# FFN of a six-stage network on one core: 512-column up products, down products two tiles behind, down weights loaded one tile later

## The chip, the cores and the metric

The kernel runs on 1 core of a Trainium2 chip. The metric is the device time in microseconds of that core. Before the change it is 1230.22 us, the median of 3 runs (1228.94 to 1235.15).

## The reference

The program is a chain of blocks on one sequence of 256 tokens with 1024 features: an attention mixer (MLA), FFN 0, a second mixer (diff), FFN 1, then FFN 2, a mixed block (sparse attention and a gated recurrence), FFN 3 and a last norm. All is in 32-bit floats. What is changed is the FFN, of which there are two kinds:

```python
def conv_ffn(x, w_up, conv_w, conv_b, w_down):   # FFN 0 and 1, 2816 hidden features
    u = x @ w_up                                  # gate half and value half side by side
    up = jnp.pad(u, ((0, 0), (1, 1), (0, 0)))
    c = conv_b
    for j in range(3):                            # 3 taps along the tokens
        c = c + conv_w[j] * up[:, j:j + s]
    g, val = c[..., :FFN_HIDDEN], c[..., FFN_HIDDEN:]
    return (jax.nn.gelu(g) * val) @ w_down

def swiglu(x, w_gu, w_down):                      # FFN 2 and 3, 2752 hidden features
    gate, up = jnp.split(x @ w_gu, 2, axis=-1)
    return (jax.nn.silu(gate) * up) @ w_down
```

## The kernel before

Every product is made of three. A 32-bit operand is split into a high part, rounded to the matmul's input type (fp32r), and a low part (the value less its high part), and `mm3` (L570 to 574) adds high·high (L572), high·low (L573) and low·high (L574) into one PSUM bank. The low·low part is left out.

An FFN runs over 22 tiles of 128 hidden features (FFN 2 and 3: the last tile has 64). In tile t:

- SP loads the up weights of the tile (`load_up`, L396: two DMAs of 512 KB, gate and value half) and the down weights (`load_down`, L409: 512 KB). `ffn` at L417 sets the order: up t, down t, up t+1, down t+1. Each load waits until the tile two before it has been split, since `raw_u` and `raw_d` have two slots each.
- ACT makes the high parts (`split_u` L1225, in the loop L1231; `split_d` L1240) and DVE the low parts (L1648, L1652). `hi_u`, `lo_u`, `hi_d` and `lo_d` have two slots.
- PE computes `up` (L659): for the gate half (s = 0) and the value half (s = 1) 8 chunks k of the 1024 features, each by `mm3`, with the weights as the stationary and the 256 tokens as the moving operand: 48 matmuls of 256 columns. The result stands in PSUM bank 4 + 2·slot + s. Tile 0 takes gate and value chunk by chunk, since it waits for the activations.
- ACT and DVE make the hidden features. FFN 0 and 1: ACT applies the middle tap and the bias from PSUM (L1300, twice), DVE the two outer taps (L1716, four times, the second of a half after its first), ACT the gelu (L1315), DVE the product with the value (L1730, again into the rounded type at L1734) and its low part (L1738). FFN 2 and 3: ACT the silu (L1307), then DVE the same three products.
- PE computes `down` (L690): 2 token tiles by 2 banks by `mm3`, 12 matmuls of 512 columns that accumulate over all tiles in banks 0 to 3. The down product of tile t comes after the up product of tile t+1 (L703 to 721).

After an FFN the result is squared and summed (ACT L1276, FFN 0 and 1), scaled and added (DVE L1688, L1692, or `add` L1700), and the next norm starts (ACT L1248, two roots on POOL L500 and L503, DVE L1664). It goes by token tile: the first waits for `first_part`, the second for the end of the last down product (`used_d`).

Each engine runs its own instruction list in order, and all order between engines is by semaphores. Tiles 2 to 19 are a loop of 9 passes over two tiles on every engine. The splits that an engine makes for a coming tile stand within the code of a tile: in tile t, ACT and DVE split the up weights of t+2 and the down weights of t+1.

Of the kernel before, what the change touches and what calls it, by code (L numbers as in the profile page):

```python
# [177 lines left out]
def program(nc, a, out):  # L178
# [12 lines left out]
    with ctx:  # L191
# [5 lines left out]
        act_hi = sb("act_hi", [P, KC, SEQ], F32R)  # L197
        act_lo = sb("act_lo", [P, KC, SEQ], F32R)
# [4 lines left out]
        hi_d = sb("hi_d", [P, 2, 1024], F32R)  # L203
        lo_d = sb("lo_d", [P, 2, 1024], F32R)
# [40 lines left out]
        cg, cv, gg, hf = (ar(512 * i, 2, SEQ) for i in range(4))  # L245

# [90 lines left out]
        d_hi, d_lo = (x[:].rearrange("p a (c t) -> p (a c) t", t=SEQ) for x in (hi_d, lo_d))  # L337
# [38 lines left out]
        def _(sp):  # L376
# [40 lines left out]
            def ffn(f):  # L417
                for t in range(2):
                    load_up(f, t, t, P)
                    load_down(f, t, t, P)  # L420
                with sp.Fori(1, LOOPED + 1) as b:
                    for t in range(2):
                        load_up(f, b * 2 + t, t, P)
                        load_down(f, b * 2 + t, t, P)
                for t in range(2 * LOOPED + 2, FT):
                    load_up(f, t, t % 2, width(f, t))
                    load_down(f, t, t % 2, width(f, t))
# [141 lines left out]
        def _(pe):  # L569
# [86 lines left out]
            def ffn(f):  # L656
                i = [N_F0, N_F1, N_F2, N_F3][f]

                def up(t, slot, n, first=False):  # L659
                    g, u = t + FT * f, t + U_OF_FFN[f]  # L660
                    unit_ready(u)
                    if not isinstance(t, int) or t >= 2:

                        if f < 2:
                            pe.wait_ge(S("tap_b"), g * 2 - 2)
                        else:
                            pe.wait_ge(S("hid_hi_done"), g - 1)
                    if n < P:

                        hi, lo = up_view(hi_u, slot, 0, 2 * n), up_view(lo_u, slot, 0, 2 * n)  # L670
                        for k in range(KC):
                            mm = mm3(psum[0:2 * n, 4 + 2 * slot, 0:SEQ], hi[:, k, :], lo[:, k, :],
                                     act_hi[:, k, :], act_lo[:, k, :], k == 0, k == KC - 1)
# [7 lines left out]
                    for s, k in order:  # L681
                        if first and s == 0:
                            pe.wait_ge(S("act_lo"), 8 * i + k + 1)
                        hi, lo = views[s]
                        mm = mm3(psum[0:n, 4 + 2 * slot + s, 0:SEQ], hi[:, k, :], lo[:, k, :],
                                 act_hi[:, k, :], act_lo[:, k, :], k == 0, k == KC - 1)
# [3 lines left out]
                def down(t, slot, n, last=False, tiles=range(TT)):  # L690
                    g = t + FT * f
                    pe.wait_ge(S("hi_d_done"), g + 1)
# [3 lines left out]
                    for tk in tiles:  # L696
                        for c in range(2):
                            w = slice(c * BANK, c * BANK + BANK)
                            mm = mm3(psum[:, 2 * tk + c, :], hid_hi[0:n, slot, tok(tk)], hid_lo[0:n, slot, tok(tk)],
                                     hi_d[0:n, slot, w], lo_d[0:n, slot, w], False, last)  # L700
                    mm.then_inc(S("used_d" if TT - 1 in tiles else "first_part"), 1)
# [19 lines left out]
                down(21, 1, width(f, 21), True, [1])  # L721
# [488 lines left out]
        def _(act):  # L1210
# [22 lines left out]
            def split_d(d, b=None):  # L1233
# [4 lines left out]
                elif d >= 2:  # L1238
                    act.wait_ge(S("used_d"), d - 1)
                act.activation(hi_d[:, d % 2, :], raw_d[:, d % 2, :], ACT.Copy).then_inc(S("hi_d_done"), 1)  # L1240
# [39 lines left out]
            def ffn(f):  # L1280
                def tile(t, slot, n, b=None):
# [4 lines left out]
                    if n < P:  # L1286
                        act.wait_ge(S("used_u"), u + 1)
                    else:

                        act.wait_ge(S("gate_up"), at(g + 1 - (f == 3)))  # L1290
                    if f < 2:

                        if looped_or_late:
                            act.wait_ge(S("hid_lo_done"), at(g - 1))
# [822 lines left out]
```

## Time and profile before

| what | value |
|---|---|
| median of 3 runs | 1230.22 us |
| the profiled execution | 1230.51 us |
| its span, first to last instruction | 1228.7 us |
| mean granted TensorE clock | 0.996 |
| PE busy | 1182.5 us, 96% of the span |
| DVE busy | 764.4 us, 62% |
| ACT busy | 599.6 us, 49% |
| bytes by DMA | 194.61 MB |

PE is a matmul's execution, PEld a weight load, DVE is VectorE, ACT ScalarE, POOL GpSimd, SP SyncE, whose queue issues the loads. In a timeline the length of a matmul counts until its result has landed, so that successive matmuls overlap: how fast PE goes is read from the distance of their starts. ACT and DVE instructions that follow one another overlap by about 0.1 us in the same way.

### The profile page before, as it was taken

Reading aid. Unit: us, or ns where it says so; the run is one execution under the profiler, and the core shown is the slowest. Engines: PE = TensorE matmul, PEld = TensorE weight load, DVE = VectorE, ACT = ScalarE, POOL = GpSimd, SP = SyncE. Lnnn points to the kernel's source line nnn. Section 1 sums busy time; section 2 is a strip of 40 time slices with the busy share of each in tenths; the row PEclk is TensorE's granted clock in tenths of the full one; section 3 lists DMA queues with packets and bytes.
Section 4 is the critical chain, followed back from the end, with each engine's and each line's share of the span. In section 5 each row is a group of like instructions: output and inputs, shape, how many; then the busy total and the mean of one; then the engine's idle time right before and its main releaser. Section 6 shows DMA issues by size and latency. Waiting matters only on the chain.

```text
span 1228.7 us, 21630 instructions
## 1 busy us (share of the span) xinstructions
PE 1182.5 (96%) x8061; PEld 1066.1 (87%) x8075; DVE 764.4 (62%) x1068; ACT 599.6 (49%) x912; POOL 66.3 (5%) x93
## 2 busy tenths in 40 slices
PE   7999999999899989999999999999999999999997
PEld 6876999999699869999988999998987777999996
DVE  5764877776656567777766554545646656555554
ACT  5454545454565655554545343335564545334342
POOL 0201000000200020000000000001000310000000
PEclk9999999999999999999999999999999999999998
DMA  6504666566344436666645665653663015766661
GB/s 203 176 35 156 205 188 193 170 200 197 103 138 138 159 117 202 192 182 178 204 137 160 184 200 177 186 163 88 196 222 116 1 35 156 211 181 197 171 178 43
DMA packets 241059, 194.61 MB, mean 158 GB/s; under 512 B 11214, under 2 KB 223792, under 8 KB 241008
## 3 DMA queue, kind: packets, MB, share of 16 engines
q1 hardware_dynamic: 240928, 193.88, 52.8%
q8 instruction: 34, 0.56, 0.2%
q14 instruction: 17, 0.14, 0.0%
q10 hardware_dynamic: 80, 0.03, 0.0%
HBM read 192.84 MB, written 1.05 MB: 158 GB/s over the span
## 4 chain that ended last, share of the span: by engine, by line
PE 86%; DVE 6%; ACT 3%; DMA 2%; POOL 1%; issue 1%; SPq 0%; POOLq 0%; ACTq 0%; DVEq 0%
PE psum L572 26%; PE psum L573 25%; PE psum L574 25%; DVE lo_u L1631 1%; PE psum L1132 1%; DMA raw_u<-in_cmp_v_w 1%; ACT hi_u L1225 1%; POOL st L503 1%; PE psum L890 1%; DVE lo_u L1648 1%; PE psum L803 1%; PE psum L804 1%; DMA raw_u<-in_mla_w_ukv 1%; POOL st L500 1%; PE psum L824 1%
## 5 line engine op out<-in xcount | busy, mean ns | idle before, releaser
L572 PE MATMUL psum<-act_hi,hi_u 128*128 128x256 f32 x1712 | 487.0, 284 | 7.7 <-DVE lo_u L1631 3.2
L574 PE MATMUL psum<-act_hi,lo_u 128*128 128x256 f32 x1712 | 484.4, 283 | 0.0
L573 PE MATMUL psum<-act_lo,hi_u 128*128 128x256 f32 x1712 | 484.4, 283 | 0.0
L1648 DVE TENSOR_TENSOR lo_u<-raw_u,hi_u 128x2048 fp32r<-128x2048 f32 (+3 forms) x122 | 273.6, 2243 | 238.7 <-ACT hi_u L1231 152.1
L572 PEld LDWEIGHTS psum<-act_hi,hi_u 128*128 128x128 f32 x1712 | 326.8, 191 | 16.1 <-issue 12.4
L573 PEld LDWEIGHTS psum<-act_lo,hi_u 128*128 128x128 f32 x1712 | 326.9, 191 | 3.3
L574 PEld LDWEIGHTS psum<-act_hi,lo_u 128*128 128x128 f32 x1712 | 326.9, 191 | 0.0
L1231 ACT ACTIVATE hi_u<-raw_u 128x2048 fp32r<-128x2048 f32 x72 | 137.7, 1913 | 88.9 <-PE psum L574 86.0
L572 PE MATMUL psum<-hi_d,hid_hi 128*128 128x512 f32 (+1 forms) x352 | 138.5, 393 | 1.4 <-DVE hid_lo L1738 1.4
L573 PE MATMUL psum<-lo_d,hid_hi 128*128 128x512 f32 (+1 forms) x352 | 138.0, 392 | 0.0
L574 PE MATMUL psum<-hi_d,hid_lo 128*128 128x512 f32 (+1 forms) x352 | 137.0, 389 | 0.0
L1300 ACT ACTIVATE arena<-psum,vecs 128x256 f32<-128x256 f32 x88 | 49.4, 564 | 176.8 <-PE psum L574 176.8
L1716 DVE SCALAR_TENSOR_TENSOR arena<-psum,vecs,arena 128x255 f32<-128x255 f32 x176 | 76.5, 477 | 75.1 <-ACT arena L1300 75.0
L1225 ACT ACTIVATE hi_u<-raw_u 128x2048 fp32r<-128x2048 f32 (+3 forms) x50 | 90.9, 1818 | 57.0 <-PE psum L574 43.9
L1240 ACT ACTIVATE hi_d<-raw_d 128x1024 fp32r<-128x1024 f32 x88 | 93.5, 1062 | 43.5 <-PE psum L574 43.4
L1652 DVE TENSOR_TENSOR lo_d<-raw_d,hi_d 128x1024 fp32r<-128x1024 f32 x88 | 107.2, 1218 | 6.4 <-ACT hi_d L1240 6.4
L572 PEld LDWEIGHTS psum<-hi_d,hid_hi 128*128 128x128 f32 (+1 forms) x352 | 66.4, 189 | 14.3 <-issue 2.9
L574 PEld LDWEIGHTS psum<-hi_d,hid_lo 128*128 128x128 f32 (+1 forms) x352 | 66.1, 188 | 14.5
L572 PE MATMUL psum<-hi_u,act_hi 128*128 128x512 f32 (+4 forms) x216 | 76.1, 352 | 0.6 <-DVE act_lo L1675 0.6
L573 PEld LDWEIGHTS psum<-lo_d,hid_hi 128*128 128x128 f32 (+1 forms) x352 | 66.4, 189 | 10.5
L573 PE MATMUL psum<-lo_u,act_hi 128*128 128x512 f32 (+4 forms) x216 | 74.5, 345 | 0.0
L574 PE MATMUL psum<-hi_u,act_lo 128*128 128x512 f32 (+4 forms) x216 | 74.3, 344 | 0.0
(232 smaller groups left out, 1224.3 us busy)
## 6 DMA issues: line engine op xcount, KB each, us to landing
raw_u<-in_ffn_w_up SPq DMA_DIRECT2D x88, 512.0 KB, 5.4
raw_d<-in_ffn_w_down SPq DMA_DIRECT2D x86, 512.0 KB, 3.5
raw_u<-in_ffn_w_gu SPq DMA_DIRECT2D x84, 512.0 KB, 5.8
raw_u<-in_diff_w_qkv SPq DMA_DIRECT2D x24, 512.0 KB, 4.6
raw_u<-in_w_in SPq DMA_DIRECT2D x24, 512.0 KB, 4.0
raw_u<-in_mla_w_o SPq DMA_DIRECT2D x8, 512.0 KB, 3.8
raw_u<-in_diff_w_o SPq DMA_DIRECT2D x8, 512.0 KB, 3.7
raw_u<-in_w_out SPq DMA_DIRECT2D x8, 512.0 KB, 4.0
```

Source lines behind the costliest of these rows:

```text
L500: pool.tensor_scalar(v, v, 1.0 / over, EPS, ALU.mult, ALU.add).then_inc(S("mean_squares"), 1)
L503: return pool.tensor_tensor(v, v, half[:, 0:n], ALU.pow)
L572: pe.matmul(o, s_hi, m_hi, start=start, stop=False)
L573: pe.matmul(o, s_hi, m_lo, start=False, stop=False)
L574: return pe.matmul(o, s_lo, m_hi, start=False, stop=stop)
L1225: act.activation(unit_view(hi_u, u), unit_view(raw_u, u), ACT.Copy).then_inc(S("hi_u_done"), 1)
L1231: act.activation(u_slot(hi_u, u0), u_slot(raw_u, u0), ACT.Copy).then_inc(S("hi_u_done"), 1)
L1240: act.activation(hi_d[:, d % 2, :], raw_d[:, d % 2, :], ACT.Copy).then_inc(S("hi_d_done"), 1)
L1300: act.activation(buf[0:n, slot, :], psum[0:n, 4 + 2 * slot + s, 0:SEQ], ACT.Identity, scale=vecs[0:n, bass.ds(w, 1)], bias=vecs[0:n, bass. ...
L1648: dve.tensor_tensor(v[0], v[1], v[2].bitcast(F32), ALU.subtract).then_inc(S("lo_u_done"), 1)
L1652: dve.tensor_tensor(lo_d[:, d % 2, :], raw_d[:, d % 2, :], hi_d[:, d % 2, :].bitcast(F32), ALU.subtract).then_inc(S("lo_d_done"), 1)
L1716: dve.scalar_tensor_tensor(buf[0:n, slot, o], psum[0:n, 4 + 2 * slot + s, x], vecs[0:n, bass.ds(w, 1)], buf[0:n, slot, o], ALU.mult, ALU.a ...
```

## The change

- `act_hi` and `act_lo` become two halves of one tensor `act_hl`, so that for a chunk k the 256 high and the 256 low columns lie side by side.
- The up product goes by `mm_beside`: one matmul of 512 columns (high weights by high and low activations; the first 256 columns of the bank get high·high, the last 256 high·low), then one of 256 columns (low weights by high activations) into the last 256. The bank then holds two partial sums side by side.
- They are added outside PE: ACT copies the right half to SBUF (`cross`), DVE adds it to the left half (`up_sum`). Taps, silu and the product with the value read `up_sum` in place of PSUM. Two such copies and sums per tile (one in the narrow last tile of FFN 2 and 3).
- The rounded hidden feature is made by ACT from `hf`, in place of DVE's second product.
- The down product of tile t comes after the up product of t+2. `hi_d` and `lo_d` get a third slot, for the last tile. At the end, both down products of the first token tile come before those of the second.
- In tile t ACT splits the down weights of t at the tile's end and DVE those of t-1 near its start. On ACT the gelu and the second middle tap now come ahead of the split of the up weights; on DVE the product with the value does.
- SP issues the down weights of t-1 behind the up weights of t.

```diff
+            def mm_beside(bank, n, s_hi, s_lo, m_hl, start, stop):
+                pe.matmul(psum[0:n, bank, :], s_hi, m_hl.rearrange("p a t -> p (a t)"), start=start, stop=False)
+                return pe.matmul(psum[0:n, bank, SEQ:], s_lo, m_hl[:, 0, :], start=False, stop=stop)
...
@@ PE, up @@
-                        if f < 2:
-                            pe.wait_ge(S("tap_b"), g * 2 - 2)
-                        else:
-                            pe.wait_ge(S("hid_hi_done"), g - 1)
+                        pe.wait_ge(S("up_sum"), g * 2 - 2)
...
@@ PE, order of the products @@
                 up(1, 1, P)
-                down(0, 0, P)
                 with pe.Fori(0, LOOPED) as b:
                     up(b * 2 + 2, 0, P)
+                    down(b * 2, 0, P)
+                    up(b * 2 + 3, 1, P)
                     down(b * 2 + 1, 1, P)
-                    up(b * 2 + 3, 1, P)
-                    down(b * 2 + 2, 0, P)
                 up(20, 0, P)
+                down(18, 0, P)
+                up(21, 1, width(f, 21))
                 down(19, 1, P)
-                up(21, 1, width(f, 21))
-                down(20, 0, P)
+                down(20, 0, P, False, [0])
                 down(21, 1, width(f, 21), True, [0])
+                down(20, 0, P, False, [1])
                 down(21, 1, width(f, 21), True, [1])
...
@@ ACT, one tile @@
+                    cross_out(0)
+                    if f < 2:
+                        conv_mid(0, cg)
+                        cross_out(1)
+                        act.wait_ge(S("tap_b"), at2(2 * g + 1))
+                        act.activation(gg[0:n, slot, :], cg[0:n, slot, :], ACT.Gelu_apprx_tanh).then_inc(S("gated"), 1)
+                        conv_mid(1, cv)
                     else:
+                        act.wait_ge(S("up_sum"), at2(2 * g + (2 if n < P else 1)))
+                        act.activation(gg[r, slot, :], up_sum[0:n, slot, 0, :], ACT.Silu).then_inc(S("gated"), 1)
+                        if n == P:
+                            cross_out(1)
                     if b is not None:
                         split_u_looped(b, u + 2)
                     elif t < 20:
                         split_u(u + 2)
+                    act.wait_ge(S("hidden"), at(g + 1))
+                    if b is not None or g >= 2:
+                        act.wait_ge(S("used_d"), at(g - 1))
+                    act.activation(hid_hi[0:n, slot, :], hf[0:n, slot, :], ACT.Copy).then_inc(S("hid_hi_done"), 1)
+                    if t + 1 < FT:
+                        split_d(g, b)
+                    if t == 20:
+                        split_d(g + 1)
...
@@ DVE, one tile @@
+                    sum_up(0)
+                    if b is not None or 0 < t < 21:
+                        split_d(g - 1, b)
                     if f < 2:
+                        taps(0, cg)
+                    if n == P:
+                        sum_up(1)
+                    if b is not None or t:
+                        hidden_low(g - 1, 1 - slot, P)
+                    dve.wait_ge(S("gated"), at(g + 1))
+                    if f < 2:
+                        taps(1, cv)
...
+                    dve.tensor_tensor(hf[0:n, slot, :], gate, val, ALU.mult).then_inc(S("hidden"), 1)
                     if b is not None or t < 20:
                         split_u(u + 2, b)
+                    if t == 20:
+                        split_d(g)
+                        split_d(g + 1)
+                    if t == 21:
+                        hidden_low(g, slot, n)
...
@@ SP, order of the loads @@
+                load_up(f, 0, 0, P)
+                for t in range(1, 4):
+                    load_up(f, t, t % 2, P)
+                    load_down(f, t - 1, (t - 1) % 2, P)
+                with sp.Fori(2, LOOPED + 1) as b:
+                    load_up(f, b * 2, 0, P)
+                    load_down(f, b * 2 - 1, 1, P)
+                    load_up(f, b * 2 + 1, 1, P)
+                    load_down(f, b * 2, 0, P)
```

## Rows read from the trace of the kernel before

**Rows 1.** The page: busy times, and the chain that ended last by engine.

```profile
PE 1182.5 (96%) x8061; PEld 1066.1 (87%) x8075; DVE 764.4 (62%) x1068; ACT 599.6 (49%) x912; POOL 66.3 (5%) x93
...
PE 86%; DVE 6%; ACT 3%; DMA 2%; POOL 1%; issue 1%; SPq 0%; POOLq 0%; ACTq 0%; DVEq 0%
```

**Rows 2.** Windows: length, PE, PEld, DVE, ACT, POOL busy, clock, DMA share, GB/s.

```profile
140.00:305.00 165.00, 165.00 (x1169) 155.55 (x1168) 117.45 (x173) 80.30 (x96) 0.00 (x0) 1.00 0.64 193
```

**Rows 3.** PE's timeline in FFN 0: start, length, line, names, shape of one matmul.

```profile
202.27 0.40 PE L572 MATMUL psum<-hi_d,hid_hi 128*128 128x512 f32 x1
202.50 0.40 PE L573 MATMUL psum<-lo_d,hid_hi 128*128 128x512 f32 x1
...
205.02 0.28 PE L572 MATMUL psum<-act_hi,hi_u 128*128 128x256 f32 x1
...
210.77 0.40 PE L572 MATMUL psum<-hi_d,hid_hi 128*128 128x512 f32 x1
```

**Rows 4.** PE's timeline elsewhere: matmuls of 280 and of 512 columns.

```profile
868.11 0.29 PE L573 MATMUL psum<-lo_u,act_hi 128*128 128x280 f32 x1
868.24 0.29 PE L574 MATMUL psum<-hi_u,act_lo 128*128 128x280 f32 x1
...
91.31 0.39 PE L572 MATMUL psum<-hi_u,act_hi 128*128 128x512 f32 x1
...
92.67 0.39 PE L572 MATMUL psum<-hi_u,act_hi 128*128 128x512 f32 x1
```

**Rows 5.** Groups by form: count, busy us, mean ns; idle time before them.

```profile
L1652 DVE TENSOR_TENSOR lo_d<-raw_d,hi_d 128x1024 fp32r<-128x1024 f32 x88 | 107.2, 1218 | 6.4 <-ACT hi_d L1240 6.4
L1240 ACT ACTIVATE hi_d<-raw_d 128x1024 fp32r<-128x1024 f32 x88 | 93.5, 1062 | 43.5 <-PE psum L574 43.4
L1307 ACT ACTIVATE arena<-psum 128x256 f32<-128x256 f32 x42 | 16.2, 385 | 72.2 <-PE psum L574 72.2
```

**Rows 6.** ACT and DVE timelines of one looped tile of FFN 0.

```profile
202.62 0.56 ACT L1300 ACTIVATE arena<-psum,vecs 128x256 f32<-128x256 f32 x1 [2.32 <-PE psum L574]
203.08 1.91 ACT L1231 ACTIVATE hi_u<-raw_u 128x2048 fp32r<-128x2048 f32 x1
203.32 1.26 DVE L1716 SCALAR_TENSOR_TENSOR arena<-psum,vecs,arena 128x255 f32<-128x255 f32 x3 [1.79 <-ACT arena L1300]
204.89 0.40 ACT L1315 ACTIVATE arena<-arena 128x256 f32<-128x256 f32 x1
205.02 2.29 DVE L1648 TENSOR_TENSOR lo_u<-raw_u,hi_u 128x2048 fp32r<-128x2048 f32 x1 [0.43 <-ACT hi_u L1231]
207.23 0.42 DVE L1730 TENSOR_TENSOR arena<-arena 128x256 f32<-128x256 f32 x1
```

**Rows 7.** Start of FFN 0: PE's zero matmuls and first down product, ACT's table load.

```profile
127.52 0.28 PE L574 MATMUL psum<-act_hi,lo_u 128*128 128x256 f32 x1
127.86 0.81 PE L707 MATMUL psum<-zeros 128*128 128x512 bf16 x3
...
134.27 0.40 PE L572 MATMUL psum<-hi_d,hid_hi 128*128 128x512 f32 x1
...
130.32 1.28 ACT L1315 ACT_TABLE_LOAD   x1
```

**Rows 8.** End of FFN 0 on PE, ACT, DVE; last, a row of the waits.

```profile
307.88 0.47 PE L572 MATMUL psum<-hi_d,hid_hi 128*128 128x512 f32 x1 [0.70 <-DVE hid_lo L1738]
...
310.97 1.02 ACT L1276 ACTIVATE junk<-psum 128x1024 f32<-128x1024 f32 x1 [0.33 <-PE psum L574]
...
314.46 1.28 DVE L1692 SCALAR_TENSOR_TENSOR resid<-normed,st,resid 128x1024 f32<-128x1024 f32 x1
...
PE psum L572 <- DVE hid_lo L1738: 1.4, 2, 0.7
```

**Rows 9.** DMA issues (KB each, median us to landing), and one late load in FFN 2.

```profile
raw_u<-in_ffn_w_up SPq DMA_DIRECT2D x88, 512.0 KB, 5.4
...
665.66 1.92 ACT L1225 ACTIVATE hi_u<-raw_u 128x2048 fp32r<-128x2048 f32 x1 [3.66 <-DMA raw_u<-in_ffn_w_gu]
```

More of the change, by code:

```diff
@@ L336, in program @@
         d_sq = junk[:].rearrange("p (b d) -> p b d", d=P)
-        d_hi, d_lo = (x[:].rearrange("p a (c t) -> p (a c) t", t=SEQ) for x in (hi_d, lo_d))
+        d_hi, d_lo = (x[:, 0:2].rearrange("p a (c t) -> p (a c) t", t=SEQ) for x in (hi_d, lo_d))
         n_q = ar(0, 4, SEQ)
@@ L417, in ffn @@
             def ffn(f):
[L418 to L424, printed above, removed]
+                load_up(f, 0, 0, P)
[7 more added lines that the diff above has]
+                    load_down(f, b * 2, 0, P)
                 for t in range(2 * LOOPED + 2, FT):
                     load_up(f, t, t % 2, width(f, t))
-                    load_down(f, t, t % 2, width(f, t))
+                    load_down(f, t - 1, (t - 1) % 2, P)
+                load_down(f, FT - 1, 1, width(f, FT - 1))
             def load_gain(i):
@@ L691, in down @@
                     g = t + FT * f
+                    d = 2 if isinstance(t, int) and t == FT - 1 else slot
                     pe.wait_ge(S("hi_d_done"), g + 1)
@@ L699, in down @@
                             mm = mm3(psum[:, 2 * tk + c, :], hid_hi[0:n, slot, tok(tk)], hid_lo[0:n, slot, tok(tk)],
-                                     hi_d[0:n, slot, w], lo_d[0:n, slot, w], False, last)
-                    mm.then_inc(S("used_d" if TT - 1 in tiles else "first_part"), 1)
+                                     hi_d[0:n, d, w], lo_d[0:n, d, w], False, last)
+                    if TT - 1 in tiles:
+                        mm.then_inc(S("used_d"), 1)
+                    elif last:
+                        mm.then_inc(S("first_part"), 1)
                 up(0, 0, P, True)
@@ new lines, in cross_out, with conv_mid @@
+                    def cross_out(part):
+                        if n < P or part:
+                            act.wait_ge(S("used_u"), at(u + 1))
+                        else:
+                            act.wait_ge(S("gate_up"), at(g + 1 - (f == 3)))
+                        act.activation(cross[:, slot, part, :], psum[:, 4 + 2 * slot + part, SEQ:], ACT.Copy)\
+                            .then_inc(S("cross_out"), 2 if n < P else 1)
+                    def conv_mid(part, buf):
+                        act.wait_ge(S("up_sum"), at2(2 * g + part + 1))
+                        w = at(V_CW + (f * 3 + 1) * 44 + part * FT + t)
+                        c = at(V_CB + f * 44 + part * FT + t)
+                        act.activation(buf[0:n, slot, :], up_sum[0:n, slot, part, :], ACT.Identity,
+                                       scale=vecs[0:n, bass.ds(w, 1)], bias=vecs[0:n, bass.ds(c, 1)])\
+                            .then_inc(S("conv_mid"), 1)
@@ new lines, in taps @@
+                    def taps(part, buf):
+                        for tap, name in ((0, "tap_a"), (2, "tap_b")):
+                            dve.wait_ge(S("conv_mid" if tap == 0 else "tap_a"), at2(2 * g + part + 1))
+                            w = at(V_CW + (f * 3 + tap) * 44 + part * FT + t)
+                            o = slice(1, SEQ) if tap == 0 else slice(0, SEQ - 1)
+                            x = slice(0, SEQ - 1) if tap == 0 else slice(1, SEQ)
+                            dve.scalar_tensor_tensor(buf[0:n, slot, o], up_sum[0:n, slot, part, x],
+                                                     vecs[0:n, bass.ds(w, 1)], buf[0:n, slot, o],
+                                                     ALU.mult, ALU.add).then_inc(S(name), 1)
```

98 lines of the change are left out of this document (33 added, 65 removed).

## The prediction

> **What bounds the kernel now.** I read the page's busy times and its chain first: PE is busy for 96% of the span and 86% of the chain that ended last is PE, the next engine has 6% [rows 1]. The window over most of FFN 0 says it more sharply: PE is busy for 165.00 of 165.00 us at full granted clock, with DVE at 117.45, ACT at 80.30 and the DMA share at 0.64 [rows 2]. So inside an FFN the time is the number of PE matmuls times the distance between their starts, and the question is what the new mix of matmuls takes, and whether DVE and ACT, which get more to do, still keep up.
>
> The distances come from PE's timeline. One tile runs from 202.27 to 210.77, 8.50 us: the down product from 202.27 to 205.02, 12 matmuls of 512 columns, 0.2292 each, and the up product from 205.02 to 210.77, 48 matmuls of 256 columns, 0.1198 each [rows 3]. At 2.4 GHz 256 columns stream in 0.1067 us and 512 in 0.2133. What a matmul costs beyond its columns is then 13.1 ns at 256 and 15.9 ns at 512; it is nearly fixed. Two other places agree: 280 columns take 0.13 (their streaming is 0.1167), and 512 columns with activations as stationary take (92.67 - 91.31) / 6 = 0.2267 [rows 4].
>
> **PE's stream.** For one chunk k the old code has three matmuls of 256, 3 x 0.1198 = 0.3594 us. The new one has one of 512 and one of 256, 0.2292 + 0.1198 = 0.3490. The columns are the same 768; what goes is one matmul's fixed part. The trace of before has no mix of the two forms, so the saving of 10.4 ns is bounded: above by the fastest 512 distance, 0.3594 - 0.2267 - 0.1198 = 12.9 ns, below by a 512 matmul that costs 0.233, as the first two of a down product may (202.27 to 202.50, at two decimals), 6.6 ns. I take 10.4, from the mean over a whole down product, the nearest row. There are 86 full tiles of 16 chunks and 2 narrow ones of 8, 1392 chunks: 14.5 us saved (9.2 to 18.0). The tile goes from 8.50 to 16 x 0.3490 + 2.75 = 8.33 us.
>
> The Trainium skill, TensorE: Matmul & The Clock Gate, section Back-to-back issue gap, gives an isolated gap of N/2.4 + 2.5 ns, by which one matmul less is worth only 2.5 ns, an estimate of 3.5 us over all chunks. The trace does not agree: the fixed part here is 13 to 16 ns.
>
> **Do DVE and ACT keep up?** The heavy case is FFN 0 and 1, with 44 tiles. Added per tile: two copies on ACT (0.39 each, as the silu from PSUM [rows 5]), one on ACT for the rounded hidden feature (0.40, as the gelu), two sums on DVE (0.42) less the dropped product (0.42). DVE goes from 117.45 / 165 x 8.50 = 6.05 us per tile to about 6.4, ACT from 4.1 to about 5.3, both under 8.33. But the work is now a chain that goes to and fro, so its length counts. I lay it out with lengths of [rows 5, 6], with an overlap of successive instructions of 0.08 on DVE (205.02 + 2.29 against 207.23) and 0.10 on ACT (202.62 + 0.56 against 203.08), and handoffs of 0.04 to 0.14 (203.18 to 203.32 is 0.14, 204.99 to 205.02 is 0.03) [rows 6]. From DVE's first sum at 0: sum to 0.34, low down weights to 1.48, first tap to 1.96, second 2.06 to 2.54; on ACT gelu 2.58 to 2.98, second middle tap 2.92 to 3.48, high up weights 3.38 to 5.29; DVE's two taps of the value and the hidden product end at 5.10 beside them; low up weights from 5.32, next tile at 7.53. So this ring takes 7.5 us by itself, 0.8 less than PE's tile.
>
> Tied to PE's times (ACT starts 0.35 after the end of an up product's last slot: 202.27 to 202.62 [rows 3, 6]): with up t starting at 0, the gate half ends at 2.79, ACT copies 3.14 to 3.53, DVE's sum starts at 3.57; the value half ends at 5.58, its copy runs 5.93 to 6.32, gelu to 6.62, value sum 6.36 to 6.78, middle tap 6.82 to 7.38, high weights to 9.19, low weights 9.22 to 11.51. DVE's next tile begins at 8.33 + 3.57 = 11.90, so 0.4 us are left; PE wants these weights at 16.67, so 5.2 us are left there. The down product of t starts at 16.67 + 5.58 = 22.2, and its operands (low hidden part and low down weights, made in tile t+1) are ready some 7 us before. ACT's rounded hidden part now waits for the down product of t-2 (end 8.33, ACT from 8.68), which is before the hidden product's end, 9.0: free. In FFN 2 and 3 there are no taps and the chain is shorter. Steady tiles: cost nothing, hidden under PE; if that cover is gone, each 0.1 us over 8.33 costs 4 us in FFN 0 and 1.
>
> **SP's order.** Up weights of t+3 now queue behind the down weights of t+1, which wait for DVE's split of the down weights of t-1, early in tile t (5.1 us after up t starts). They are wanted by ACT at about 7.3 + 8.33 = 15.6, 10.5 us later. A load lands in 5.4 us by the median, and the worst wait in the FFN 2 start was 3.66 for one [rows 9]; even 8 us would fit. The DMA share of 0.64 [rows 2] goes to 0.65. Cost nothing.
>
> **Start of each FFN.** Before, down 0 (2.75 us) stood between up 1 and up 2. Now up 2 follows up 1 at once, and its weights are split only after tile 0's features. Before, up 0 ends at 127.64 (127.52 + 0.12), and up 1 ends at 134.27 [rows 7]; after, up 0 ends 0.17 earlier and up 1 0.34 earlier, at 133.93. The chain of tile 0: value half copied from 127.8, but the gelu's table load, 1.28 us [rows 7], which before lay behind the split of the up weights, now stands ahead of it: copy to 129.09 (it queues behind the gate's middle tap), table to 130.35, gelu to 130.77, middle tap to 131.23, high weights 131.13 to 133.04, low weights to 135.35, PE from 135.5. That is a new stall of 1.6 us (2.5 if the table load waits for the taps, 0.3 if it is done early), in FFN 0 and 1. In FFN 2 and 3 the same chain without taps and middle taps is ready 0.1 us after up 1 ends. Sum 3.4 us (1 to 5.5). Tile 3 and on: the ring, started late by about 4 us, gains 0.8 per tile and PE has 5 us of slack, so no more stalls.
>
> **End of each FFN.** Before, PE waits 0.70 us for the last low hidden part, in two FFNs, 1.4 in all [rows 8]. After, 4.1 us of down products cover it instead of 2.75, but the part is made later: DVE has two down splits (2 x 1.22 [rows 5]) in tile 20, so tile 21's first sum starts at 12.7 instead of 11.9 (up 20 at 0), its hidden product ends at 17.4, rounded and low part at 18.3, PE 18.4 against 18.04: a stall of 0.4. Saved 0.3 x 2 = 0.6 (-0.6 to +1.4). Behind it, the first token tile is finished 2.75 us before PE's end instead of 1.37. Before, the second's last step starts at 314.46, 3.8 after PE's end (307.88 + 2.75, about 310.7), bound by DVE's row of four long instructions. After, the first two are done by then and the second waits for its own square (310.97 + 1.22) and its root, about 1.9 us more: 3.4 after PE's end. 0.4 us saved in each of FFN 0 and 1, sum 0.8; in FFN 2 and 3 the one step of the second token tile is on the path as before: nothing.
>
> **The sum**, made against the profiled execution: 1230.5 - 14.5 + 3.4 - 0.6 - 0.8 = 1218.0 us. The profiled execution is 0.3 us above the median, so the same against the median: 1218. With the bounds of the unknown terms: 1212 to 1224.
>
> **Rivals.**
> - *The fixed part isn't saved.* If the 512 matmul in this mix costs what two of 256 do, 0.2396, PE's stream stays as it is and only the starts and ends count: 1230.5 + 3.4 - 1.4 = 1232.5; by half of it 1225. The Trainium skill's gap formula, named above, would put it at 1229, by an estimate. Against: 512 columns take 0.2292 and 0.2267 [rows 3, 4]. For: no row has the mix, with a narrow and a wide matmul in turn behind a weight load each. Chance 0.13.
> - *Slower: DVE and ACT become the bound in FFN 0 and 1.* The place is the ring of 7.5 us. It decides once it is longer than 8.33: its about 8 handoffs would each have to cost 0.1 us more than I took, for instance since each new wait in the loop is against a computed count. At 8.9 us it costs 0.57 x 40 looped and late tiles = 23 us: 1218 + 23 = 1241. For: 0.4 us of slack is thin, and handoffs are seen at 0.14. Against: the old loop shows none beyond it. Chance 0.10.
> - *PE gains more*, by the fastest distance and with starts that cost little: 1230.5 - 18.0 + 1 - 1.4 = 1212 and below. Chance 0.10.
> - *The change doesn't do what it says*: loads that land late through SP's new order. They would show as ACT waiting for DMA, and cost PE only beyond 5 us: no price of its own; with a late load in every start, 2 to 4 us, inside the forecast's upper part.
>
> **Chances.** Forecast (1212 to 1224) 0.67, fixed part not saved 0.13, DVE and ACT bound 0.10, more gain 0.10. A measurement of this kernel can tell about 0.5%, 6 us, from no change. Faster by over 0.5% (below 1224): 0.67 + 0.10 = 0.77; within 0.5%: 0.13 and a little of the ring's mild form, 0.14; slower: 0.09. The range 1210 to 1229 takes in the forecast, most of the higher gain and the cheaper part of the first rival, and leaves out 2 in 10.
>
> **What would show it.** Starts of a 512 and the next matmul in an up product 0.229 apart, then 0.120; looped tiles of 8.33 us in all four FFNs with PE busy throughout. The first rival shows as tiles of 8.5 with PE busy, the second as tiles above 8.4 in FFN 0 and 1 alone, with PE waiting for DVE's low up weights. Stalls of 1.6 us ahead of up 2 in FFN 0 and 1, of about 0.4 ahead of the last down products. I am wrong if the looped tile is not between 8.28 and 8.40.

## The result and the profile after

| | before | after |
|---|---|---|
| median of 11 runs | 1230.50 us (1228.54 to 1238.59) | 1225.23 us (1220.93 to 1228.64) |
| span of the profiled execution | 1228.7 us | 1223.3 us |
| PE busy | 1182.5 us | 1177.0 us |
| DVE, ACT busy | 764.4, 599.6 us | 808.0, 692.6 us |

The ratio is 0.9939, with a 95% interval of 0.9917 to 0.9961. By the ratio the change is worth 7.5 us (4.8 to 10.2), by the medians 5.3, where 12.5 were forecast. The median of 1225.23 lies inside the range of 1210 to 1229, but just above the forecast proper of 1212 to 1224.

The page of the changed kernel, the counterpart of [rows 1]: busy times, and the chain by engine.

```profile
PE 1177.0 (96%) x6669; PEld 992.3 (81%) x6683; DVE 808.0 (66%) x1154; ACT 692.6 (57%) x1174; POOL 64.1 (5%) x93
...
PE 84%; DVE 6%; ACT 4%; DMA 3%; issue 1%; POOL 1%; SPq 1%; POOLq 0%; ACTq 0%; DVEq 0%
```

PE still bounds the kernel, with 1392 matmuls fewer. Its timeline in FFN 0, against [rows 3]:

```profile
199.83 0.40 PE L581 MATMUL psum<-hi_d,hid_hi 128*128 128x512 f32 x1
...
202.22 0.40 PE L587 MATMUL psum<-act_hl,hi_u 128*128 128x512 f32 x1
202.45 0.28 PE L588 MATMUL psum<-act_hl,lo_u 128*128 128x256 f32 x1
202.57 0.40 PE L587 MATMUL psum<-act_hl,hi_u 128*128 128x512 f32 x1
202.81 0.28 PE L588 MATMUL psum<-act_hl,lo_u 128*128 128x256 f32 x1
...
207.52 0.40 PE L581 MATMUL psum<-hi_d,hid_hi 128*128 128x512 f32 x1
...
215.90 0.40 PE L581 MATMUL psum<-hi_d,hid_hi 128*128 128x512 f32 x1
```

A tile takes 215.90 - 207.52 = 8.38 us (8.387 as the mean of the looped ones), not 8.33. The up product, which starts at 201.88, takes 5.64 and not 5.58: 0.3525 us a chunk, about 0.235 for the wide matmul and 0.1175 for the narrow one. That single number is nearly all of what the forecast missed inside the FFNs.

DVE's timeline of one tile there:

```profile
196.92 0.43 DVE L1743 TENSOR_TENSOR arena<-psum,arena 128x256 f32<-128x256 f32 x1 [0.22 <-ACT arena L1311]
...
201.28 1.11 DVE L1753 SCALAR_TENSOR_TENSOR arena<-arena,vecs 128x255 f32<-128x255 f32 x2 [0.78 <-ACT arena L1319]
202.43 0.42 DVE L1781 TENSOR_TENSOR arena<-arena 128x256 f32<-128x256 f32 x1
202.80 2.29 DVE L1678 TENSOR_TENSOR lo_u<-raw_u,hi_u 128x2048 fp32r<-128x2048 f32 x1
```

DVE comes back to its first sum 0.22 us before ACT's copy is there. So PE paces DVE, as forecast, but by half the slack that I had laid out.

PE's longest waits in the changed kernel (total, times, longest):

```profile
PE psum L613 <- DVE normed L1695: 10.9, 11, 2.2
...
PE psum L587 <- DVE lo_u L1678: 3.1, 2, 1.6
```

The two waits for `lo_u` are new: they stand before the third up product of FFN 0 and FFN 1. The waits for `hid_lo` of [rows 8] are no longer in this list, but a late start is left at the same place:

```profile
304.08 0.47 PE L581 MATMUL psum<-hi_d,hid_hi 128*128 128x512 f32 x1
```

This is the first matmul of down 21 in FFN 0. It starts 0.43 us behind the one before it (303.65), where 0.23 is usual, and DVE's low hidden part is done only at 303.93. The next distance is 0.30, so about 0.28 us are lost, for 0.94 before. FFN 1 has the same.

**The difference by stretch**, from the starts of PE's first up product and the end of its last down product in each FFN:

| stretch | before | after | difference |
|---|---|---|---|
| FFN 0 | 188.91 | 187.41 | -1.50 |
| FFN 1 | 188.87 | 187.51 | -1.36 |
| FFN 2 | 185.30 | 183.33 | -1.97 |
| FFN 3 | 185.30 | 183.30 | -2.00 |
| FFN 1 to FFN 2 | 11.08 | 9.42 | -1.66 |
| mixed block, FFN 2 to FFN 3 | 197.78 | 202.43 | +4.65 |
| all else | 271.5 | 269.9 | -1.6 |

The FFNs gain 6.8 us. The mixed block, which the change does not touch, is 4.65 us longer, and its windows show why (columns as in [rows 2]):

```profile
829.59:929.59 100.00, 94.89 (x687) 85.40 (x687) 58.48 (x79) 54.00 (x70) 2.32 (x4) 1.00 0.61 181
929.59:949.59 20.00, 18.24 (x88) 12.16 (x88) 11.68 (x29) 11.33 (x46) 5.18 (x3) 0.79 0.13 50
949.59:969.59 20.00, 20.00 (x127) 14.72 (x125) 11.12 (x31) 10.04 (x40) 4.37 (x5) 0.95 0.00 1
...
941.40:951.60 10.20, 10.20 (x33) 6.41 (x33) 4.24 (x11) 3.03 (x14) 2.94 (x2) 0.50 0.00 0
```

The granted clock is 0.79 over 20 us; a closer window has it at 0.50, the lower of its two levels (1.2 GHz for 2.4), for some 10 us. Whether that belongs to the change was the first question. Of the 1.6 us in "all else", 0.96 lie ahead of FFN 0 (its first up product starts at 120.85 after 121.81), in code that the change does not touch, and 0.56 behind FFN 3.

### The profile page after: what moved, and what is told of

Same layout as the page of the kernel before. It is cut to its first block, busy times and chain, and to the rows that moved or that the text cites. A ratio compares the mean times of both kernels' runs of the same rounds, so it can differ in the third digit from the quotient of the medians.

```text
span 1223.3 us, 19144 instructions
## 1 busy us (share of the span) xinstructions
PE 1177.0 (96%) x6669; PEld 992.3 (81%) x6683; DVE 808.0 (66%) x1154; ACT 692.6 (57%) x1174; POOL 64.1 (5%) x93
## 4 chain that ended last, share of the span: by engine, by line
PE 84%; DVE 6%; ACT 4%; DMA 3%; issue 1%; POOL 1%; SPq 1%; POOLq 0%; ACTq 0%; DVEq 0%
PE psum L587 26%; PE psum L588 13%; PE psum L581 12%; PE psum L582 12%; PE psum L583 12%; DVE lo_u L1661 2%; PE psum L1148 1%; DMA raw_u<-in_cmp_v_w 1%; ACT hi_u L1241 1%; DVE lo_u L1678 1%; ACT hi_u L1238 1%; DMA raw_u<-in_diff_w_qkv 1%; PE psum L906 1%; PE psum L1105 1%; PE psum L819 1%
## 5 line engine op out<-in xcount | busy, mean ns | idle before, releaser
L587 PE MATMUL psum<-act_hl,hi_u 128*128 128x512 f32 x1392 | 495.7, 399 | 4.4 <-DVE lo_u L1678 3.1
L588 PE MATMUL psum<-act_hl,lo_u 128*128 128x256 f32 x1392 | 390.3, 280 | 0.0
L587 PEld LDWEIGHTS psum<-act_hl,hi_u 128*128 128x128 f32 x1392 | 261.5, 188 | 70.6 <-issue 7.1
L588 PEld LDWEIGHTS psum<-act_hl,lo_u 128*128 128x128 f32 x1392 | 262.8, 189 | 3.1
L1311 ACT ACTIVATE arena<-psum 128x256 f32<-128x256 f32 x174 | 66.2, 380 | 168.0 <-PE psum L588 167.7
L1743 DVE TENSOR_TENSOR arena<-psum,arena 128x256 f32<-128x256 f32 x174 | 73.5, 423 | 111.8 <-ACT arena L1311 111.8
L1753 DVE SCALAR_TENSOR_TENSOR arena<-arena,vecs 128x255 f32<-128x255 f32 x176 | 84.9, 483 | 43.8 <-ACT arena L1319 32.7
L581 PE MATMUL psum<-act_hl,hi_u 128*128 128x256 f32 (+1 forms) x320 | 92.3, 288 | 5.9 <-DVE lo_u L1661 3.6
L582 PE MATMUL psum<-act_hl,hi_u 128*128 128x256 f32 (+1 forms) x320 | 90.3, 282 | 0.0
L583 PE MATMUL psum<-act_hl,lo_u 128*128 128x256 f32 (+1 forms) x320 | 90.3, 282 | 0.0
L581 PE MATMUL psum<-hi_u,act_hl 128*128 128x512 f32 (+4 forms) x216 | 76.2, 353 | 0.8 <-DVE act_hl L1706 0.8
```

What stands on the lines that cost most here:

```text
L581: pe.matmul(o, s_hi, m_hi, start=start, stop=False)
L582: pe.matmul(o, s_hi, m_lo, start=False, stop=False)
L583: return pe.matmul(o, s_lo, m_hi, start=False, stop=stop)
L587: pe.matmul(psum[0:n, bank, :], s_hi, m_hl.rearrange("p a t -> p (a t)"), start=start, stop=False)
L588: return pe.matmul(psum[0:n, bank, SEQ:], s_lo, m_hl[:, 0, :], start=False, stop=stop)
L1743: dve.tensor_tensor(up_sum[:, slot, part, :], psum[:, 4 + 2 * slot + part, 0:SEQ], cross[:, slot, part, :], ALU.add).then_inc(S("up_sum"), ...
```

## The experiments

Unless said otherwise, each kernel is the changed one with the edit shown. The theory at the start: the up product is slower than 5.58 us since a wide and a narrow matmul follow one another singly. The rivals: a wide matmul with up weights costs 0.235 wherever it stands; or high and low weights in turn cost it.

**The kernel before, once more** (no edit).

> The kernel before, once more, for its own trace of the mixed block. If the clock dip in the changed kernel's mixed block (0.79 of full clock over 20 us) is chance, it can show here as well and costs some 5 us; if only the change brings it on, the granted clock stays at 1.00 in every window of the block and the span is 1228 to 1229 us.

Measured: 1233.4 us in one run, span 1231.6. Its mixed block:

```profile
836.20:936.20 100.00, 95.68 (x693) 86.08 (x693) 59.45 (x81) 56.17 (x74) 3.27 (x5) 1.00 0.60 183
936.20:956.20 20.00, 18.24 (x85) 12.12 (x83) 10.87 (x28) 10.52 (x44) 5.30 (x3) 0.77 0.10 40
```

The dip is there without the change, at the same place, and the block takes 201.6 us with it. In the trace of the early table load below the same stretch is at 1.00 and takes 197.1. So the dip comes with some executions of either kernel, costs 4 to 5 us, and the profiled pair had it on one side only. Its FFNs took 188.91, 188.87, 185.30 and 185.30, the same as in the first trace: lengths of FFNs compare, spans do only with their dips. What decides in which execution it comes stays open.

**Groups of eight.**

In every tile but the first, and but the narrow last one of FFN 2 and 3, the loop over the chunks one by one is replaced:

```diff
+                        for s in range(2):
+                            hi, lo = views[s]
+                            for k in range(KC):
+                                pe.matmul(psum[0:n, 4 + 2 * slot + s, :], hi[:, k, :],
+                                          act_hl[:, k].rearrange("p a t -> p (a t)"), start=k == 0, stop=False)
+                            for k in range(KC):
+                                mm = pe.matmul(psum[0:n, 4 + 2 * slot + s, SEQ:], lo[:, k, :], act_hl[:, k, 0, :],
+                                               start=False, stop=k == KC - 1)
```

> Changed kernel, but in every up product after tile 0 a half's 8 matmuls of 512 columns come first and its 8 of 256 after them, in place of one and one in turn. Theory A (the turn from wide to narrow and back costs 3.5 ns a chunk): a wide one takes 0.229 and a narrow one 0.120, the up product 5.58 us in place of 5.64, the tile 8.33, in all 4 to 5 us less than the changed kernel. Theory B (what a matmul costs beyond its columns is not fixed, and 512 columns out of the activations with up weights as stationary cost 0.235 wherever they stand): the up product stays at 5.64 and the time is the same.

Measured: 1217.09 us, ratio 0.9898 (0.9861 to 0.9936). The FFNs take 735.7 us together, against 741.6 for the changed kernel. One up product:

```profile
199.86 1.98 PE L696 MATMUL psum<-act_hl,hi_u 128*128 128x512 f32 x8
201.67 1.11 PE L699 MATMUL psum<-act_hl,lo_u 128*128 128x256 f32 x8
202.63 2.00 PE L696 MATMUL psum<-act_hl,hi_u 128*128 128x512 f32 x8
204.47 1.12 PE L699 MATMUL psum<-act_hl,lo_u 128*128 128x256 f32 x8
205.42 0.40 PE L581 MATMUL psum<-hi_d,hid_hi 128*128 128x512 f32 x1
```

The first loop is the high weights by high and low activations, the second the low weights by the high ones. Eight wide ones take 1.81 and 1.84 us, 0.228 each, eight narrow ones 0.95, 0.119 each: the up product is 5.56 us. The same matmuls on the same operands, in another order, are 5 ns a chunk faster. The rival that a wide one costs 0.235 wherever it stands has fallen.

**Groups of two**, run once and then again with more runs (edit as above, with `for k in (k0, k0 + 1)` in place of the loops over all k).

> Changed kernel with the matmuls of two chunks grouped: two of 512 columns, two of 256, and so on. One in turn gave an up product of 5.64 us (32 changes of width), groups of eight 5.56 (4 changes). If each change of width costs the same, 2.9 ns, this one (16 changes) lies half way, 5.59 to 5.60. If only the direct succession of single ones costs (each weight load behind a matmul of the other width), groups of two are already at 5.56; if long groups are needed, it stays at 5.64.

> The groups of two once more, now timed: the changed kernel with this edit alone. Its four FFNs are 6.9 us shorter than the changed kernel's (734.7 against 741.6) by the profiles, so about 1216 to 1218 if only that counts. If single executions scatter by dips of the clock outside the FFNs, its times spread by up to 5 us above its best while tiles stay at 8.29.

Measured: 1214.53 us in the single run; 1217.08 as the median of six, ratio 0.9881 (0.9851 to 0.9911). The six run from 1212.60 to 1220.17, a wider spread than the 5 us expected. The tile is 8.29 us:

```profile
202.46 0.63 PE L697 MATMUL psum<-act_hl,hi_u 128*128 128x512 f32 x2
202.93 0.39 PE L700 MATMUL psum<-act_hl,lo_u 128*128 128x256 f32 x2
203.16 0.62 PE L697 MATMUL psum<-act_hl,hi_u 128*128 128x512 f32 x2
...
207.34 0.40 PE L581 MATMUL psum<-hi_d,hid_hi 128*128 128x512 f32 x1
...
215.63 0.40 PE L581 MATMUL psum<-hi_d,hid_hi 128*128 128x512 f32 x1
```

The up product takes 5.56 us, no more than with groups of eight, though there are 16 changes of width for 4, and the down product behind it takes 2.73 for 2.75. So the cost does not go by the number of changes: a pair is enough to get rid of the 5 ns a chunk. The wide matmuls are not quicker by themselves: the pair at 202.46 takes 0.235 each, the narrow pair behind it 0.115 each. What falls is the sum, 0.695 us for two chunks where 0.705 was the sum one by one.

**Both matmuls wide.**

```diff
-                return pe.matmul(psum[0:n, bank, SEQ:], s_lo, m_hl[:, 0, :], ...)
+                return pe.matmul(psum[0:n, bank, :], s_lo, m_hl.rearrange("p a t -> p (a t)"), ...)
```

> Changed kernel with the second matmul of a chunk at 512 columns too (low weights by high and low activations; it adds the low by low part, which the others leave out). The stationary operand still goes high, low, high, low, one by one, but all matmuls have one width. If the change of width is what made single alternation slow (0.3525 us a chunk against 0.3466 in groups of two), a matmul takes 0.226 to 0.229 here, as in the groups and the down product, and the up product 7.25 to 7.33 us. If the alternation of high and low weights is what costs, whatever the width, it takes 0.232 to 0.235, 7.42 to 7.52 us.

Measured: 1361.02 us in one run.

```profile
204.44 0.39 PE L581 MATMUL psum<-hi_d,hid_hi 128*128 128x512 f32 x1
...
207.16 0.39 PE L587 MATMUL psum<-act_hl,hi_u 128*128 128x512 f32 x1
...
214.41 0.39 PE L581 MATMUL psum<-hi_d,hid_hi 128*128 128x512 f32 x1
```

32 wide matmuls in 7.25 us, 0.2266 each, with high and low weights in turn one by one. So turning between the two weight tensors is free; the width in turn is what costs. Even the down product is quicker here, 2.72 for 2.75: with no narrow matmul ahead of it, all its distances are 0.2267 too. The cause inside PE, below the width, stays open.

**Three narrow matmuls.**

```diff
-                pe.matmul(psum[0:n, bank, :], s_hi, m_hl.rearrange("p a t -> p (a t)"), start=start, stop=False)
+                pe.matmul(psum[0:n, bank, 0:SEQ], s_hi, m_hl[:, 0, :], start=start, stop=False)
+                pe.matmul(psum[0:n, bank, SEQ:], s_hi, m_hl[:, 1, :], start=False, stop=False)
```

> Changed kernel with the one matmul of 512 columns undone: high weights by high activations (256 columns, left half of the bank) and high weights by low activations (256, right half), then the third as before; all else of the change stays. If only the 512-column matmul speeds PE up: up product back at 5.75 us, tile at 8.50, and the FFNs 9.9 us longer than the changed kernel's, 1230 to 1235 in all, no better than before. If order, loads or the new work of ACT and DVE brought the gain, it stays near 1224.

Measured: 1234.21 us, ratio 1.003 (1.0008 to 1.0052).

```profile
206.80 0.40 PE L581 MATMUL psum<-hi_d,hid_hi 128*128 128x512 f32 x1
...
209.55 0.28 PE L587 MATMUL psum<-act_hl,hi_u 128*128 128x256 f32 x1
...
215.30 0.40 PE L581 MATMUL psum<-hi_d,hid_hi 128*128 128x512 f32 x1
```

The tile is back at 8.50 and the FFNs take 751.2 us, 9.7 more than the changed kernel and 2.9 more than before. Inside the FFNs all the gain of the change is in the wide matmul. The rest of it costs 2.9 us there: 3.4 in the starts and 0.8 in passages between 128 and 64 rows, less 1.3 at the ends. The whole is slower than before by 0.3%.

**The table load early.**

```diff
+                act.activation(early[:, f:f + 1], vecs[:, 0:1], ACT.Gelu_apprx_tanh if f < 2 else ACT.Silu)
                 tile(0, 0, P)
```

> Changed kernel plus one one-column gelu (silu) on ACT at the start of each FFN, so that ACT's table load of 1.28 us is done while it waits for the first up product. My working has the load on the chain to the weights of tile 2: the stall before the third up product falls from 1.6 us to 0.3 in FFN 0 and 1 and the 0.17 in FFN 2 and 3 goes, 2.7 us in all. The rival, that the loads of the weights or DVE's own work set that stall, leaves it at 1.6.

Measured: 1219.99 us, ratio 0.9916 (0.9886 to 0.9946). PE waits 1.11 us before the third up product, after 1.60; the FFNs take 740.0 us, 1.5 less than the changed kernel, where 2.7 were expected. Most of what else the profiled executions differ by is the mixed block, 5.3 us shorter here with its clock at 1.00. ACT's timeline shows what is late next:

```profile
121.20 1.28 ACT L1351 ACT_TABLE_LOAD   x1
...
127.32 0.42 ACT L1329 ACTIVATE arena<-arena 128x256 f32<-128x256 f32 x1 [0.81 <-DVE arena L1755]
```

The gelu now waits 0.81 us for DVE's taps. I had written a saving of 1.3 us for a load of 1.28, without asking what the gelu waits for besides.

**The order of the last down products undone.**

```diff
-                down(20, 0, P, False, [0])
-                down(21, 1, width(f, 21), True, [0])
-                down(20, 0, P, False, [1])
+                down(20, 0, P)
+                down(21, 1, width(f, 21), True, [0])
```

> Changed kernel with the order of the last down products undone: down 20 for both token tiles, then down 21 for the first, then for the second. All 12+12 matmuls are the same; the first token tile is then finished 1.37 us before PE's end, not 2.75. If that order is what shortened the stretch from FFN 1's last down product to FFN 2's first up product (11.08 us before, 9.42 after), it goes back to about 11 there and by as much behind FFN 0, and the whole is 1 to 2 us slower than the changed kernel. If POOL's scatter made it (its short instructions take 0.19 or 1.2 us), the stretch stays near 9.4 to 10 and the time is the same.

Measured: 1225.73 us, ratio 0.9957 (0.9931 to 0.9984), against 0.9939 (0.9917 to 0.9961) for the changed kernel: the totals don't tell them apart. The stretch from FFN 1 to FFN 2 does, in windows from the last down product to the first up product (before, changed, order undone; columns as in [rows 2]):

```profile
640.76:651.84 11.08, 8.71 (x39) 5.07 (x40) 9.34 (x10) 6.46 (x10) 5.80 (x8) 0.85 0.00 1
636.84:646.26 9.42, 7.26 (x39) 3.85 (x40) 8.06 (x9) 6.47 (x11) 3.98 (x6) 1.00 0.00 1
637.99:648.52 10.53, 7.33 (x40) 3.85 (x40) 9.25 (x10) 6.46 (x11) 5.80 (x8) 1.00 0.00 1
```

At full clock the order is worth 1.1 us here. The remaining 0.55 of the 1.66 between before and after is the clock, 0.85 in this stretch of the kernel before (and again in its second trace, 11.23 us). Scatter of POOL's instructions did not make it: every trace of a kernel with the new order, eleven of them, has 9.42 or 9.43. Behind FFN 3 the order is worth another 0.55 us (8.48 with it undone, 7.94 with it).

Behind FFN 0 it gains only 0.1, and a row of ACT in the changed kernel shows why:

```profile
305.07 2.01 ACT L1238 ACTIVATE hi_u<-raw_u 128x1024 fp32r<-128x1024 f32 x2 [1.60 <-DMA raw_u<-in_diff_w_qkv]
```

ACT splits the first weights of the next mixer ahead of the square of the first token tile, and here it waits 1.60 us for their load. From the end of PE's last down product to PE's first transpose of the normed values it takes 6.44 us, after 6.56 before; where ACT doesn't wait, as behind FFN 1 and, with both matmuls wide, behind FFN 0, it is 5.20.

Against it stands what happens in FFN 2 and 3, where tile 21 has only 64 features:

```profile
824.61 0.39 PE L583 MATMUL psum<-hi_d,hid_lo 128*128 128x512 f32 x1
824.93 0.49 PE L581 MATMUL psum<-hi_d,hid_hi 64*128 64x512 f32 x1
825.26 0.39 PE L582 MATMUL psum<-lo_d,hid_hi 64*128 64x512 f32 x1
```

These rows are the changed kernel's. The two distances around the first 64-row matmul are 0.32 and 0.33 where 0.23 is usual. Each passage between 128 and 64 rows costs 0.2 us, and the new order has three of them for one. With the order undone FFN 2 takes 182.87 us, 0.46 less, and FFN 0 and 1, where down 21 then starts on time, 0.2 and 0.4 less.

**SP's order undone** (up t, down t, up t+1, down t+1, as in the kernel before).

> Changed kernel with SP's order undone: up t, down t, up t+1, down t+1. The down weights of t+1 then hold back the up weights of t+2 until DVE has split the down weights of t-1, which the change has moved into tile t, the very tile in which ACT splits the up weights of t+2. From DVE's first sum of a tile: down load issued at 1.5, up load at 2 to 3, landed at about 8.5, split by ACT to 10.4 and by DVE to 12.6, against 8.39 per tile. Theory (the order is needed for the late down splits): tiles of 12 to 13 us, 1500 to 1560 us in all. Rival (two slots of weights give enough slack): within 10 us of the changed kernel.

Measured: 1618.46 us in one run, above the 1500 to 1560 expected. ACT's waits:

```profile
ACT hi_u L1244 <- DMA raw_u<-in_ffn_w_gu: 287.3, 36, 9.2
ACT hi_u L1244 <- DMA raw_u<-in_ffn_w_up: 201.2, 36, 6.2
```

DVE's low up weights, one per tile, start at 240.07, 253.76 and 267.73, 13.8 us apart where 12.6 was worked out. The clock, 0.92 over a run in which PE often stands still, may be part of that; how much isn't shown. The later load of the down weights is no gain by itself, but without it the later down splits would cost 390 us.

**The distance of the down product undone** (down t right after up t+1).

> Changed kernel with PE's order alone undone: the down product of t right after the up product of t+1. Its operands (low hidden part of t) are made by DVE in tile t+1, about 7.3 us after up t+1 starts, while up t+1 ends at 5.6. Theory (the second tile of distance is what hides the longer chain over ACT and DVE): a stall of 1.7 us before each down product, tiles of 10.1 us, about 1360 us. Rival (the chain was short enough for one tile): tiles stay at 8.39 and the time near 1222.

Measured: 1365.64 us in one run, tiles of 9.97:

```profile
209.99 0.47 PE L581 MATMUL psum<-hi_d,hid_hi 128*128 128x512 f32 x1 [1.35 <-DVE hid_lo L1760]
219.96 0.47 PE L581 MATMUL psum<-hi_d,hid_hi 128*128 128x512 f32 x1 [1.35 <-DVE hid_lo L1760]
```

The wait of 1.35 us per tile, and slow first matmuls behind it, is what the second tile of distance hides.

**A first try at a better version:** groups of two, and the up weights of tiles 2 and 3 split before the taps of tiles 0 and 1.

```diff
                     cross_out(0)
+                    early_split = b is None and t < 2
+                    if early_split:
+                        cross_out(1)
+                        split_u(u + 2)
```

(and DVE's split after its two sums.)

> A version meant to beat both: the groups of two, and in tiles 0 and 1 of each FFN the split of the up weights of tiles 2 and 3 ahead of the taps, gelu (silu) and hidden product, on ACT and DVE. Steady tile 8.29 as with the groups alone. The stall before the third up product, 1.6 us in FFN 0 and 1 and 0.17 in FFN 2 and 3, should go, since the weights are then ready 1.5 us ahead; what is late next is tile 3's weights and the first down product, with about 1 us to spare by my working. In all 3 to 3.5 us under the groups alone (1214.5 in one run), 1211 to 1213; if tile 1's chain then falls behind, part of it comes back as a stall before the fourth up product.

Measured: 1226.90 us, ratio 0.9936 (0.9909 to 0.9962): 7 us worse than the groups of two alone by the ratios, where 3 better were expected. The wait before the third up product is gone, FFN 2 and 3 take 181.5 and 181.4 us. But in FFN 0 and 1 the taps of tiles 0 and 1 now stand behind a split, and the second down product waits (in FFN 0 the fifth up product too, 1.68 us):

```profile
482.69 0.47 PE L581 MATMUL psum<-hi_d,hid_hi 128*128 128x512 f32 x1 [2.02 <-DVE hid_lo L1777]
...
484.19 0.63 PE L582 MATMUL psum<-lo_d,hid_hi 128*128 128x512 f32 x1
484.62 0.63 PE L583 MATMUL psum<-hi_d,hid_lo 128*128 128x512 f32 x1
```

Behind that wait in FFN 1 the matmuls start 0.43 apart for some 3 us, where the granted clock is 0.50 (483.10 to 486.50). That isn't a sure result of the stall: in FFN 0 PE waits the same 2.02 us ahead of the same product, and the clock behind it stays at 1.00. The four FFNs take 739.9 us, 5.2 more than with the groups of two alone; the rest of the loss lies outside them, in a stretch between FFN 0 and 1 that is 2.9 us longer and in a dip of the mixed block.

**The second try:** groups of two, the early table load, and the early split in FFN 2 and 3 alone.

> The groups of two, the early table load, and the early split of the up weights of tiles 2 and 3 in FFN 2 and 3 alone, where no taps wait behind it. From the FFN lengths seen: FFN 0 and 1 go from 185.7 (groups of two) by the 0.5 us of the early table load to 185.2, FFN 2 and 3 to 181.4, all four 733 us against 734.7 for the groups alone and 741.6 for the changed kernel. Steady tile 8.29. About 8 us faster than the changed kernel. If the early split again leaves a later stall, it shows ahead of the first three down products of FFN 2 and 3.

Measured: 1214.50 us, ratio 0.9873 (0.9836 to 0.9909). The FFNs take 185.22, 185.14, 181.48 and 181.38, in all 733.2, as worked out. It beats both kernels; over the groups of two alone (0.9881) its 1.5 us of FFN are inside the scatter of whole runs.

## Why the prediction was right or wrong

| step | forecast | measured |
|---|---|---|
| PE's stream, 1392 chunks | -14.5 | -9.7 (7.0 ns a chunk) |
| starts | +3.4 | +3.4 (1.60, 1.51 and twice 0.17) |
| ends | -0.6 | -1.3, and +0.8 for the passages between 128 and 64 rows |
| behind FFN 0 and 1 | -0.8 | -1.7 behind FFN 1 (order -1.1, clock -0.6), -0.1 behind FFN 0 |
| behind FFN 3 | 0 | -0.6 |
| ahead of FFN 0 | 0 | -1.0, in code that the change leaves alone |
| clock in the mixed block | not foreseen | +4.7 in the profiled execution |

**PE's stream: the mechanism right, the size off.** The wide matmul saves time, and it alone: with three narrow ones the tile is 8.50. The step that failed is the saving per chunk, 10.4 ns for 7.0: the term was 4.8 us too large. I took the distance of a wide matmul, 0.2292, as the mean over a whole down product, and put none of it down to the matmuls ahead. Two more rows of the kernel before, from the down product of [rows 3], show what that mean is made of:

```profile
202.74 0.39 PE L574 MATMUL psum<-hi_d,hid_lo 128*128 128x512 f32 x1
...
203.66 0.39 PE L572 MATMUL psum<-hi_d,hid_hi 128*128 128x512 f32 x1
```

The first two wide matmuls, right behind the narrow ones of the up product, take 0.235 each (202.27 to 202.74), and the last six 0.2267 (203.66 to 205.02). The first is the distance that the mix then had, the second the one of a stream without narrow ones. So the trace of before did hold the succession in question. I read its bad end off one distance, 202.27 to 202.50, as 0.233 and put the floor at 6.6 ns; by the first two it is 4.6, and the 7.0 measured lies between that and the forecast. In groups a chunk takes 0.3474 to 0.3477, about 1.5 ns less than the 0.3490 forecast. The rule that I weighed beside it from the Trainium skill, TensorE: Matmul & The Clock Gate, section Back-to-back issue gap, with 2.5 ns for each matmul beyond its columns, does not hold for this stream: the settled distances of 0.120 and 0.2267 are 13 ns beyond the columns at both widths.

**DVE and ACT keep up: right.** The ring worked out at 7.53 us; where it runs by itself, at the start of FFN 0, DVE's timeline has the low up weights of two tiles 7.49 apart:

```profile
132.14 2.29 DVE L1678 TENSOR_TENSOR lo_u<-raw_u,hi_u 128x2048 fp32r<-128x2048 f32 x1 [0.27 <-ACT hi_u L1241]
...
139.63 2.29 DVE L1678 TENSOR_TENSOR lo_u<-raw_u,hi_u 128x2048 fp32r<-128x2048 f32 x1 [0.27 <-ACT hi_u L1241]
```

In the steady tile 0.22 us of slack were left of the 0.4 laid out. The rival in which they become the bound did not come, but the first try at a better version, where PE waits 2.02 us once a split stands ahead of the taps, shows how near it is once one thing is moved.

**The starts: right in sum and in place,** 1.60 us where 1.6 was written, by the chain that was written. The remark beside it, 0.3 with an early table load, was wrong: it gives 1.11, since the taps end late.

**SP's order costs nothing: right,** and the experiment gives what the order is worth.

**The ends: a passage missed.** Ahead of down 21 in FFN 0 and 1, 0.28 us are lost where a stall of 0.4 was forecast, and 0.94 before: right in place. But the new order of the last down products makes two more passages between 128 and 64 rows in FFN 2 and 3, a cost that stood in the trace of before, once in each of these two, and that I had not looked for. Behind the FFNs the order gains more than the 0.4 of the forecast where nothing else holds ACT (1.1 behind FFN 1), and 0.6 behind FFN 3, where I had put nothing.

**The total.** FFNs: -11.7 forecast, -6.8 measured, nearly all of it the stream. The profiled execution took 1225.1 us for the 1218.0 forecast: 4.8 from the stream and 4.7 from the clock's dip in the mixed block, less 2.5 that other stretches gained beyond the forecast. A third of the stream's term was lost, which is a part of the first rival. That its half version had 1225 and the median is 1225.23 is luck, since the clock put some 5 us on top that no version had. The upper end of 1224 was narrow as well: the bounds of the terms, added up, give 1227. The dips scatter single executions: the runs of the changed kernel with a mean granted clock of 0.996 took 1221 to 1223 us, those at 0.991 took 1228 to 1229.

## What to carry to other kernels

When matmuls of two widths must alternate, put them in groups of at least two of a width: the same work was 5 ns a chunk quicker here, which is 7 us of FFN time on top of the 9.7 of the wide matmul. A distance between starts holds for the sequence it was read in: don't take the mean over a product, read the matmuls right behind a change of width, which may be in the trace already. Before a gain is put down to a change, ask for the granted clock of the stretch on both sides. And when a chain to and fro over two engines gets longer, what keeps it free is the distance of its consumer and the order of the loads, not its busy time: each undone, they cost 140 and 390 us here, and neither shows in a busy share. Last, where an engine's next job stands in a fixed order behind a load, a shorter path ahead of it can end in a wait for that load, as ACT's behind FFN 0.

## What the runs showed of the hardware

Matmul starts in a stream: 0.120 us for 256 columns and 0.2267 for 512, each among its like. Behind narrow matmuls the first two wide ones take 0.235 each; when the two widths alternate singly it is 0.235 and 0.1175, 5 ns more a chunk than in groups of two or eight. Turning between two weight tensors at one width costs nothing. Passages between products of 128 and of 64 rows: 0.2 us each. In the mixed block the same instructions had a granted clock of 1.00 throughout in some executions and of 0.50 for some 10 us in others, with PE busy for 18.24 or 18.25 of the 20 us around its fall in all of them, so that PE's busy share did not tell which it would be. A wait of PE of 2.02 us was followed by the lower clock in one FFN and not in another.
